# A conformer block followed by a macaron block on one core: the filler matmuls behind the norms' statistics are left out

## What is computed

```python
# first block, layer 0 has the convolution, layer 1 the attention
for i in range(2):
    mix = conformer_conv(x) if i == 0 else stick_breaking_attention(x) @ wo
    x = layer_norm(ALPHA * x + mix)                                 # mix0, mix1
    ffn = (silu(causal_conv3(x @ w_gate)) * (x @ w_up)) @ w_down    # 1024 -> 2816 -> 1024
    ple = sigmoid(x @ ple_gate) * (p[i] @ ple_proj)
    x = layer_norm(ALPHA * x + ffn + ple)                           # ffn0, ffn1
# second block
x = x + 0.5 * rms(swiglu(rms(x)))          # ff1_pre, ff1_post
x = x + rms(hybrid_mixer(rms(x)))          # mix_pre, mix_post
x = x + 0.5 * rms(swiglu(rms(x)))          # ff2_pre, ff2_post
```

## Time and profile before

| | |
|---|---|
| median of 3 executions | 2717.21 us (2716.81 to 2722.59) |
| the profiled execution, own time | 2716.55 us |
| its span | 2714.6 us |
| TensorE matmuls busy | 2591.8 us, 95% |
| VectorE, ScalarE, GpSimd busy | 36%, 34%, 33% |
| mean granted clock of TensorE | 0.974 |

### The profile page before, as it was taken

One profiled execution on the slowest core, in us unless ns is written; L12 is line 12 of the kernel. 1 busy time (PEld: TensorE's weight loads), 2 busy tenths in 40 slices (PEclk: granted clock), 3 DMA queues, 4 the chain that ended last, 5 costly groups with the idle time before them and its releaser, 6 DMA issues.

```text
span 2714.6 us, 30924 instructions
## 1 busy us (share of the span) xinstructions
PE 2591.8 (95%) x11090; PEld 1957.5 (72%) x11090; DVE 978.2 (36%) x1304; ACT 933.9 (34%) x1424; POOL 909.2 (33%) x373
## 2 busy tenths in 40 slices
PE   8889999999999999999999999998998999999997
PEld 6536788888677767888885888875665446688886
DVE  7985344410522232444104333015234442433302
ACT  4224333322556533333224222222223333422212
POOL 2212444444322234444442444432221002244442
PEclk9999999999999999999999999999998779999999
DMA  3101232322111122322321232331110001123232
GB/s 135 57 20 62 80 106 93 100 93 93 63 55 55 39 70 93 95 98 94 98 94 55 93 100 94 93 131 70 47 55 24 8 8 55 62 93 99 95 93 77
DMA packets 57057, 206.64 MB, mean 76 GB/s; under 512 B 6304, under 2 KB 6304, under 8 KB 56736
## 3 DMA queue, kind: packets, MB, share of 16 engines
q1 hardware_dynamic: 56016, 199.96, 22.7%
q10 hardware_dynamic: 976, 5.77, 0.5%
HBM read 203.61 MB, written 2.10 MB: 76 GB/s over the span
## 4 chain that ended last, share of the span: by engine, by line
issue 64%; POOL 21%; PE 13%; DVE 1%; POOLq 0%; DMA 0%; SPq 0%; ACT 0%; DVEq 0%
POOL wL L340 21%; PE ps L378 4%; PE ps L380 4%; PE ps L379 4%; DMA raw<-ws 0%; POOLq L339 0%; POOLq L345 0%; DVE tmp L1511 0%; DVE tmp L1519 0%; DVE xf L1522 0%; SPq L310 0%; DVE x_squares L1503 0%; PE ps L469 0%; PE ps L466 0%; ACT wH L895 0%
## 5 line engine op out<-in xcount | busy, mean ns | idle before, releaser
L340 POOL TENSOR_TENSOR wL<-raw,wH 128x1024 fp32r<-128x1024 f32 x369 | 909.0, 2465 | 1773.1 <-ACT wH L895 1773.1
L378 PE MATMUL ps<-xH,wH 128*128 128x512 f32 x2104 | 836.7, 398 | 42.8 <-DVE xL L1338 10.8
L380 PE MATMUL ps<-xH,wL 128*128 128x512 f32 x2104 | 823.2, 391 | 0.0
L379 PE MATMUL ps<-xL,wH 128*128 128x512 f32 x2104 | 823.1, 391 | 0.0
L895 ACT ACTIVATE wH<-raw 128x1024 fp32r<-128x1024 f32 x371 | 392.8, 1059 | 1153.4 <-PE ps L380 1144.0
L378 PEld LDWEIGHTS ps<-xH,wH 128*128 128x128 f32 x2104 | 397.5, 189 | 150.9 <-issue 20.3
L379 PEld LDWEIGHTS ps<-xL,wH 128*128 128x128 f32 x2104 | 397.7, 189 | 84.4 <-issue 4.0
L380 PEld LDWEIGHTS ps<-xH,wL 128*128 128x128 f32 x2104 | 397.3, 189 | 84.2
L378 PE MATMUL ps<-hH,wH 128*128 (+1 forms) x704 | 277.7, 394 | 3.5 <-DVE tmp L1405 3.5
L380 PE MATMUL ps<-hH,wL 128*128 (+1 forms) x704 | 276.0, 392 | 0.0
L379 PE MATMUL ps<-hL,wH 128*128 (+1 forms) x704 | 273.2, 388 | 0.0
(11 more groups left out here) (230 smaller groups left out, 2257.4 us busy)
## 6 DMA issues: line engine op xcount, KB each, us to landing
raw<-ws SPq DMA_DIRECT2D x371, 512.0 KB, 3.5
w1b<-w ACTq DMA_DIRECT2D x2, 2048.0 KB, 11.4
xf<-xT SPq DMA_DIRECT2D x8, 256.0 KB, 7.2
out<-xf SPq DMA_DIRECT2D x8, 256.0 KB, 2.0
pf<-pT ACTq DMA_DIRECT2D x2, 512.0 KB, 4.3
con<-consts SPq DMA_DIRECT2D x1, 637.0 KB, 7.2
par<-params SPq DMA_DIRECT2D x1, 564.5 KB, 8.2
ropeT<-rope ACTq DMA_DIRECT2D x1, 512.0 KB, 4.2
```

Source lines behind the costliest of these rows:

```text
L340: pool.tensor_tensor(wL[:, j, :], raw[:, j, :], fp(wH[:, j, :]), ALU.subtract).then_inc(low_ready, 1)
L378: pe.matmul(bank, wH[:, slot, cols], rh, start=start, stop=False)
L379: pe.matmul(bank, wH[:, slot, cols], rl, start=False, stop=False)
L380: return pe.matmul(bank, wL[:, slot, cols], rh, start=False, stop=stop)
```

## The change

The two calls of `keep_warm` behind the statistics go; nothing else is touched. `sumsq_product` is called five times and `post_sumsq` twice with a name other than ff2_post, so 5 x 18 + 2 x 26 = 142 matmuls go. The 46 in the attention stay.

```diff
@@ -468,13 +468,10 @@
                     pe.wait_ge(squared, 8 * NORM[name] + n + 1)
                     mm = pe.matmul(ps[1][:], cc("mean"), squares[:, n, :], start=False, stop=n == KT - 1)
                 mm.then_inc(sumsq, 8)
-                if name != "ff2_post":
-                    keep_warm(7, 26)
 
             def sumsq_product(name, bank):
                 for n in range(KT):
                     one_square(name, n, bank)
-                keep_warm(7, 18)
 
             def ffn(inst, xname, ple_tiles=0):
                 c0 = CHUNK[f"gateup{inst}"]
```

## The result

The changed kernel is slower by 0.3%: 2726.32 us in the median of 20 executions (2718.77 to 2731.43) against 2716.64 us (2708.80 to 2724.30) for 20 of the kernel before on the same chips. The ratio is 1.0029 with a 95% interval of 1.0019 to 1.0039, which is +7.9 us (5.2 to 10.6). The ratio is not the quotient of the two medians, which lie 9.7 us apart; the means lie 7.8 us apart. The forecast was +5.95 us on the profiled execution. Both kernels scatter by 13 to 16 us, far more than the three runs shown before had suggested.

The account below looks back on a forecast made before the run. The prediction took TensorE, busy 95% of the span, as the bound: its speed and short waits. Terms 1.6 + 4.05 + 0.3 = +5.95 us on 2716.55 us gave 2722.5 us, range 2717.5 to 2728.5 us.

Parts of the forecast that it names:

- Direct price 0 us: At all seven sites, removing 24.2 us of filler work gains 0 us, because the norm's own chain takes the whole stretch.
- Each of the seven pauses, of 4.3 us and more, costs the clock: Behind all seven norm sites, idle stretches of 4.5 to 6.9 us are followed by half clock, about 3.4 us.
- conf, +1.6 us: Behind conf, TensorE is the bound from the first tile on, so a low-clock stretch costs its full 1.6 us.
- mix0, ffn0, mix1, +1.35 us each, 4.05 us: Behind these three, 1.6 us lost less 0.25 us of slack waiting for VectorE: 1.35 us each, together +4.05 us.
- rival 4: Luck with other pauses, two of 2.19 us included: 1.6 us per place either way, spreading all cases 2 to 3 us; no own chance.
- The last three, +0.3 us: Behind ffn1, ff1_post and mix_post the clock already falls; it may begin earlier, booked at 0.1 us each.
- The sum, 5.95 us: Whole kernel: 1.6 + 4.05 + 0.3 = +5.95 us on the profiled 2716.55 us, giving 2722.5 us.
- Rival 1: At the seven sites, the clock costs nothing more than now: +0.3 us, 2717 us; chance 0.12.
- Rival 2: Each new fall at the early four sites lasts as long as the 6.70 us row: +11.7 us, 2728 us; chance 0.1.
- a sign of being wrong: Low-clock stretches behind the early sites lasting 6 us and more would show the prediction wrong.
- Rival 3: Behind ff1_post and mix_post, a VectorE/GpSimd overlap dissolves, giving back 1.5 us each; chance 0.1, 0.03 of it really faster.
- The mean clock: Over the whole kernel, the mean granted clock would fall from 0.974 to about 0.972.

Follow-up runs that it names:

- the first experiment: Kernel before with bursts removed only behind ffn1, ff1_post and mix_post: 2717.73 us against 2716.81, ratio 1.0007.
- the kernel with the misplaced burst: Kernel before with all seven bursts lengthened and five more added, one of 29 behind the hybrid mixer's third item: 2719.08 us against 2716.81, ratio 1.0009.
- the longer bursts: Kernel before with all seven bursts lengthened to 25 to 40 matmuls, ending just before the next product: 2716.42 us against 2716.81, ratio 1.0003.
- the moved burst: The kernel with the misplaced burst, its burst of 29 made 28 behind the fourth item: 2714.06 us against 2716.12 for the kernel before, 0.9987.
- the fillers behind the means: Kernel with the moved burst plus 8 fillers between mean and squares of each layer norm: 2709.78 us against 2717.36 for the kernel before, 0.9968.

## Why the prediction was right, point by point

- **Direct price 0 us: right.** The "go" stages are the same to 0.2 us with bursts of 0, 4, 9, 18 or 25 to 40 matmuls. The three exceptions in all profiled executions (15.25 and 13.65 us at ff1_post, 14.80 at conf, instead of 13.1 and 12.75) had the clock at 0.50 during the squares themselves. At ff1_post it fell there in nine other executions too, but within 0.5 us of the first square, and the stage took at most 13.2 us; in the two exceptions there it fell 1.1 and 1.3 us after it. The cover is the norm's own chain.
- **Each of the seven pauses, of 4.3 us and more, costs the clock: right.** All seven sites fell in both executions of the changed kernel. The general reading behind it, that pauses of 3.3 us and more all do, is too strong: the pause of 3.32 us in the changed kernel was not followed by a fall.
- **conf, +1.6 us: open.** A stretch of 3.4 us at 0.50 costs 1.6 us there, as worked out: 52.4 us instead of 50.8, in the second execution of the kernel before and in the first experiment. In the two of the changed kernel the stage is 2.8 us over its undisturbed length, with the clock low for 4.6 and 6.2 us. By the prediction's own rate the second is 2.9 us, which fits. The first is 2.2 us; the rest lies in products that stand 0.233 us apart up to the end of the stage, at a granted clock of 1.00, instead of 0.229 us as in all other executions, and no run shows why. But the kernel before falls there too at times, at 1.6 us, and with conf alone out the whole was +0.0 us (-3.5 to +3.5).
- **mix0, ffn0, mix1, +1.35 us each, 4.05 us: the term that was too small.** With these three alone out, +6.5 us (3.5 to 9.5) were measured. Where the fall was short, 3.1 to 3.4 us, the stages behind mix0 and mix1 grew by only 1.0 to 1.1 us, less than the 1.35 booked. Three things were missing in the term. The low stretch was taken as 3.4 us, and it was up to 5.8; at 5.4 to 5.8 us the cost was 2.0 to 2.2 us. The fall at the pause of 3.32 us behind ffn0 became longer, so that this stage grew by 2.1 to 2.2 us in four of five executions. And the later pauses of 2.19 us were counted as luck that hits both kernels alike (rival 4 of the prediction). In the profiled executions they cost 1.5 to 1.6 us in 9 of 10 cases without the bursts and in 4 of 10 with them, which over two pauses is 1.6 us more.
- **The last three, +0.3 us: not told apart from it.** The measured +1.9 us (-0.8 to +4.9) holds both 0.3 and 0; behind ffn1 the low stretch grew to 5.6 us in one execution.
- **The sum, 5.95 us: right in size and sign,** with 7.9 us (5.2 to 10.6) measured. That it came so near is in part luck: the early three were worth 2.4 us more than booked, and conf, at +0.0 us, perhaps 1.6 us less.
- **The rivals.** Rival 1, no more falls than now, would need no change behind mix0, and there is one. Rival 2, long low stretches, was half right: 4.6 to 6.2 us occur, and 6.2 us behind conf is beyond the 6 us that the prediction had named as a sign of being wrong. Rival 3, a collision that dissolves, did not happen: TensorE still waits 1.51 us behind ff1_post in the changed kernel. Behind mix_post it waits 1.03 us instead of 1.54, but only because it arrives later: the product that waits starts 10.8 us after the first one of its stage, against 10.3 before. The mean clock was forecast at 0.972 and was 0.965; part of the difference is low clock inside the pauses, where nothing runs (0.68 to 0.78 in some of them), and part is the hybrid mixer.
- **What stays open.** The hybrid mixer took 473.8 us in both executions of the changed kernel and 469.6 and 470.2 in those of the kernel before, but 466.2 to 472.6 in five others with some early bursts missing or all shortened. Whether the change lengthens it on average is not settled. The prediction had no term for it.

The Trainium skill, "TensorE: Matmul & The Clock Gate", section "HAM oscillation — how this bites in real kernels", advises against idle gaps between bursts of matmuls. The pauses of 4.3 us and more above agree with it: in the two profiled executions of the changed kernel 14 falls stand behind 14 pauses.

## What to carry to other kernels

Filler matmuls in a pause that other engines set cost nothing and are worth about 1 to 2 us per pause here, even at half their length; judge them by the clock of the stage behind the pause, not by the busy share. Before adding one, read from the timeline which product really waits there and for how long: the same burst one item too early cost 4 us. Where executions of one kernel scatter by 15 us, compare stages of several profiled executions, since a single pair of them can show 9.4 us where 7.9 are true, 4.2 of them in a stage where the share of the change is not settled.

## What the runs showed of the hardware that was not expected

- **The clock falls under a busy engine too.** In the hybrid mixer of the kernel with the misplaced burst TensorE worked without a pause, most of the time on score products of 64 rows, and the clock fell and stayed at 0.50 for 13.7 us:

```profile
1953.86:1957.27 3.41, 3.41 (x12) 1.46 (x11) 0.69 (x1) 1.06 (x1) 2.13 (x1) 1.00 0.50 154
1957.27:1960.69 3.42, 3.42 (x6) 1.03 (x5) 1.17 (x2) 0.00 (x0) 0.20 (x1) 0.50 0.00 0
1960.69:1964.10 3.41, 3.41 (x7) 1.21 (x6) 2.40 (x6) 0.94 (x3) 0.00 (x0) 0.50 0.00 0
```

  In the kernel before the same products ran at 1.00 there. The same stretch of 13.7 us stands in three more profiled executions, those with the longer bursts, with the moved burst and with the fillers behind the means. Further on in the mixer the kernel before does it too: TensorE is busy throughout and the clock is at 0.50 for 10.2 and for 13.7 us, among others. The last waits before these two falls, of 0.27 and 0.36 us, had ended 5.1 and 2.9 us earlier:

```profile
2100.09:2110.33 10.24, 10.24 (x20) 3.69 (x19) 4.68 (x17) 4.29 (x16) 0.00 (x0) 0.50 0.00 1
...
2147.88:2161.53 13.65, 13.65 (x28) 5.22 (x28) 5.52 (x17) 4.29 (x16) 0.00 (x0) 0.50 0.01 2
```

  Of the 145.7 us that its clock is low, 105.8 us lie between the product behind ff1_post and the first square of mix_post, most of them in the mixer. A filler has no pause to fill in the two stretches shown.
- **The mixer's time follows its time at low clock.** Over thirteen profiled executions, all but the one with the misplaced burst, it took 466.2 us with 99.0 us at 0.50 (twice), 468.8 us with 105.3 us (once), 469.2 to 469.7 us with 105.8 us (four times), 470.2 to 470.5 us with 109.2 us (three times), 472.6 us with 113.0 us (once), and 473.8 us with 116.5 us (twice): 7.6 us between the ends, for 17.5 us more at 0.50, so 0.43 us for each us at 0.50, near the 0.47 of the full products. The 7.6 us are about half of the scatter of the executions.
- **Falls come in step.** The distance of 54.6 us from the rise behind mix0 to the next fall, the same in five executions, is described above; behind mix1 it is 54.6 us as well in the four of them that have a second fall there.
